# Hyena stage: both directions' filters multiplied once in two halves of the array, their sum and difference formed on VectorE, and the weights' low parts subtracted on GpSimd

## The reference, cut to what matters

```python
def hyena_mixer(h, w_in, b_in, short_w, short_b, w1, b1, w2, b2, w3, freq, filt_bias, w_out, b_out):
    L = h.shape[1]
    u = centred_depthwise_conv(h @ w_in + b_in, short_w, short_b)
    v, x1, x2 = jnp.split(u, 3, axis=-1)
    filt = hyena_filters(L, w1, b1, w2, b2, w3, freq)
    z = x1 * two_sided_fft_conv(v, filt[:, 0, 0], filt[:, 0, 1], filt_bias[0])
    z = x2 * two_sided_fft_conv(z, filt[:, 1, 0], filt[:, 1, 1], filt_bias[1])
    return z @ w_out + b_out
```

## Time and profile before

| | us |
|---|---|
| median of three executions | 2646.16 |
| lowest, highest | 2643.12, 2646.53 |
| the profiled execution's own time | 2648.7 |
| its span | 2646.3 |
| PE busy | 2461.9 (93%) |
| DVE busy | 1141.1 (43%) |
| ACT busy | 773.5 (29%) |
| POOL busy | 51.5 (2%) |

### The profile page before, as it was taken

How to read it: one execution, slowest core, us unless ns; L and a number is a source line. 1 busy time by engine, 2 the same in 40 slices (tenths; PEclk the granted TensorE clock), 3 DMA queues, 4 the chain that set the end, 5 groups by cost and what they waited for, 6 DMA issues and landing times. The chain is left out here.

```text
span 2646.3 us, 39564 instructions
## 1 busy us (share of the span) xinstructions
PE 2461.9 (93%) x16812; PEld 1555.6 (59%) x16812; DVE 1141.1 (43%) x2226; ACT 773.5 (29%) x1602; POOL 51.5 (2%) x68
## 2 busy tenths in 40 slices
PE   8989999999899999978799999998999969988887
PEld 7856888888678888855443334344767743322222
DVE  4456543333788989886300000002556542211113
ACT  4346433333433333223311111112347522110002
POOL 0000000000000000000200000000000010000000
PEclk9979999999999999987899999999999979999999
DMA  5240332222210101025799999997230479999996
GB/s 205 97 153 29 143 116 96 96 96 96 94 50 33 50 33 50 32 112 203 313 383 397 377 384 386 393 384 320 101 159 2 191 258 367 428 428 428 427 428 284
DMA packets 58103, 570.49 MB, mean 216 GB/s; under 512 B 6815, under 2 KB 15015, under 8 KB 24776
## 3 DMA queue, kind: packets, MB, share of 16 engines
q1 hardware_dynamic: 50904, 544.37, 51.5%
q0 software_dynamic: 5584, 18.35, 2.2%
q10 hardware_dynamic: 1440, 5.24, 0.5%
HBM read 554.84 MB, written 13.11 MB: 215 GB/s over the span
## 5 line engine op out<-in xcount | busy, mean ns | idle before, releaser
L2973 PE MATMUL moe_gate<-ring,moe_xe_l 128*32 128x512 f32 (+1 forms) x1240 | 192.6, 599 | 17.8 <-DMA ring<-in_moe_gu 11.9
L3960 DVE SCALAR_TENSOR_TENSOR moe_hidden<-moe_hidden,moe_gate_rows,moe_up 128x512 f32<-128x512 f32 x31 | 23.2, 747 | 400.4 <-ACT moe_hidden L3883 400.4
L2973 PE MATMUL moe_up<-ring,moe_xe_l 128*32 128x512 f32 (+1 forms) x1240 | 190.2, 594 | 0.0
L3988 DVE SCALAR_TENSOR_TENSOR residual<-experts_psc,mod,residual 128x512 f32<-128x512 f32 (+1 forms) x76 | 53.3, 707 | 283.9 <-PE experts_psc L3824 169.1
L3744 PE MATMUL experts_py_l<-ring,experts_turn_l 128*32 128x512 f32 (+1 forms) x1136 | 141.3, 593 | 3.5 <-DMA ring<-in_moe_down 2.8
L1019 DVE TENSOR_TENSOR mlp_w_lo<-ring,mlp_w_hi 128x512 fp32r<-128x512 f32 x144 | 96.7, 688 | 97.8 <-ACT mlp_w_hi L964 97.6
L3883 ACT ACTIVATE moe_hidden<-moe_gate 128x512 f32<-128x512 f32 x31 | 18.5, 597 | 360.2 <-PE moe_up L2973 360.2
L964 ACT CAST mlp_w_hi<-ring 128x512 fp32r<-128x512 f32 x144 | 86.4, 618 | 123.5 <-PE mlp_acc L920 123.5
L2973 PEld LDWEIGHTS moe_up<-ring,moe_xe_l 128*32 128x32 f32 (+1 forms) x1240 | 49.7, 115 | 108.2 <-issue 108.2
L2973 PEld LDWEIGHTS moe_gate<-ring,moe_xe_l 128*32 128x32 f32 (+1 forms) x1240 | 44.8, 115 | 99.9 <-issue 70.1
L918 PE MATMUL mlp_acc<-mlp_h_hi,mlp_w_hi 128*128 128x512 f32 x256 | 100.0, 391 | 0.0
(11 more groups left out here) (678 smaller groups left out, 5210.5 us busy)
## 6 DMA issues: line engine op xcount, KB each, us to landing
ring<-in_moe_gu SPq DMA_DIRECT2D x91, 2048.0 KB, 11.3
ring<-in_moe_down SPq DMA_DIRECT2D x45, 2048.0 KB, 9.8
ring<-in_ada_w SPq DMA_DIRECT2D x24, 2048.0 KB, 8.6
ahead_wide_early<-in_moe_gu SPq DMA_DIRECT2D x9, 2048.0 KB, 30.5
ahead_wide_high<-in_moe_gu SPq DMA_DIRECT2D x9, 2048.0 KB, 30.5
ahead_wide_low<-in_moe_gu SPq DMA_DIRECT2D x9, 2048.0 KB, 30.4
normed<-in_moe_gu SPq DMA_DIRECT2D x9, 2048.0 KB, 30.5
ring<-in_w_up SPq DMA_DIRECT2D x8, 2048.0 KB, 7.4
```

Of the source, the lines that this page charges most:

```text
L2973: last = core.nc.tensor.matmul(banks[m][at:at + n, :], xe_l[:, e, k, a:a + n], columns(2 * kk + m, FH * half, FH), start=(k == 0), stop=(k ...
```

## The change

- **Filters.** `w3` becomes [128, 2, 256]: forward weights in rows 0 to 63, backward in rows 64 to 127. `filters` takes two tiles at a time and issues four products of 64 rows and 256 columns: for each tile one in the upper and one in the lower half of the array, with two banks, one for the forward and one for the backward filter.
- **Taps.** `make_taps` multiplies two tiles of one direction in one operation (six operations of 512 elements per order, as before). The new function `sides` forms the sum, then the difference as -2 times the backward taps plus the sum, both in place and linked, and adds the bias row on one partition. It is called for taps 0 to 3 and for taps 4 and 5.
- **Waits.** A counter `taps_made` (four a turn) takes the place of `sp_free` for what needs the finished taps: the first unit of `transform` waits for the first call of `sides`, the third unit for the second. SP's reloads wait for it too. TensorE's `filters` wait for `win_loaded` instead of for ScalarE.
- **ScalarE.** `turn_filters_round` goes; its four uses with it.
- **Low parts.** `weights_low` for turns 0 and later (36 subtractions of 128x512) moves from VectorE's program to GpSimd's queue: pieces 4 and 5 of the turn before at the head of a turn, pieces 0 to 3 behind the wait for `project(it - 1, 5)` and, from turn 1 on, for `outwards(it - 1)`.
- **SP.** One DMA less per turn (four instead of five, and `at_zero`).

```diff
-w3 = st.sb("w3", [P, 2, 2, QC])
+w3 = st.sb("w3", [P, 2, QC])
...
-turned_round = st.counter("hy_filters_turned_round", TURNS)
+taps_made = st.counter("hy_filters_turned_round", 4 * TURNS)
...
-win_loaded = st.counter("hy_win_loaded", 96 * TURNS)
+win_loaded = st.counter("hy_win_loaded", 80 * TURNS)
...
+def taps_at(it, o, first):
+    return taps_made.at(4 * it + 2 * o + (2 if first else 1))
...
         for q in range(TURNS):
...
-                sp.wait_ge(sp_free.handle, sp_free.at(4 + spec_at(q - 1, 18 + 5)))
+                sp.wait_ge(taps_made.handle, taps_at(q - 1, 1, 4))
             last_layer = ins["hy_ffn_w3_2"].rearrange("a (o d c) -> a o d c", o=2, d=2)[:, :, :, q * QC:(q + 1) * QC]
             sp.dma_start(win[:], core.consts["window"][:, :, q * QC:(q + 1) * QC]).then_inc(win_loaded.handle, 16)
             for s in range(2):
-                sp.dma_start(w3[0:64, :, s, :], last_layer[:, :, 0, :]).then_inc(win_loaded.handle, 16)
-            sp.dma_start(w3[64:P, :, 0, :], last_layer[:, :, 1, :]).then_inc(win_loaded.handle, 16)
+                sp.dma_start(w3[64 * s:64 * (s + 1), :, :], last_layer[:, :, s, :]).then_inc(win_loaded.handle, 16)
             sp.dma_start(at_zero[:], ins["hy_bias_rows"][:, 0, q * QC:(q + 1) * QC]).then_inc(win_loaded.handle, 16)
             if q == 0:
...
-            sp.wait_ge(sp_free.handle, sp_free.at(4 + spec_at(q, 5)))
+            sp.wait_ge(taps_made.handle, taps_at(q, 0, 4))
             sp.dma_start(at_zero[:], ins["hy_bias_rows"][:, 1, q * QC:(q + 1) * QC]).then_inc(win_loaded.handle, 16)
...
         def filters(it, o, some=range(6)):
-            for t in some:
-                b = take_spec(it, 18 * o + t)
-                nc.tensor.matmul(b[:], h2[:, t * P:(t + 1) * P], w3[:, o].rearrange("p s n -> p (s n)"), start=True, stop=True).then_inc(sp_done.handle, 1)
-
-        def transform(it, m0, src):
+            for t in some[::2]:
+                both = [take_spec(it, 18 * o + t + s) for s in range(2)]
+                for i in range(2):
+                    for s in range(2):
+                        side = slice(64 * s, 64 * (s + 1))
+                        last = nc.tensor.matmul(both[s][:, i * QC:(i + 1) * QC], h2[side, (t + i) * P:(t + i + 1) * P], w3[side, o, :], start=True, stop=True, tile_position=(64 * s, 0))
+                        if i:
+                            last.then_inc(sp_done.handle, 1)
+        def transform(it, m0, src, made):
...
+                    if a == 0 and s in made:
+                        pe.wait_ge(taps_made.handle, made[s])
...
         def spectra(it, o):
-            pe.wait_ge(sp_free.handle, sp_free.at(4 + spec_at(it, 18 * o + 5)))
-            transform(it, 18 * o + 6, lambda a: taps[:, a])
+            transform(it, 18 * o + 6, lambda a: taps[:, a], {0: taps_at(it, o, 0), 2: taps_at(it, o, 4)})
...
             if it == 0:
-                pe.wait_ge(turned_round.handle, turned_round.at(1))
+                pe.wait_ge(win_loaded.handle, win_loaded.at(64))
                 filters(0, 0)
...
             if full:
-                pe.wait_ge(turned_round.handle, turned_round.at(it + 2))
+                pe.wait_ge(win_loaded.handle, win_loaded.at(80 * (it + 1) + 64))
                 filters(it + 1, 0, range(4))
...
+        def weights_low(it, i):
+            for half in range(2):
+                pool.wait_ge(w_high.handle, w_high.at((it + 1) * 2 * NP + 2 * i + half + 1))
+                n = chunk(it, i)
+                nc.gpsimd.tensor_tensor(piece(core.slot_low(n), i, 4 * half, 4), piece(core.slot(n), i, 4 * half, 4), w_hi[:, (2 * i + half) % W_BUFS],
+                                        ALU.subtract).then_inc(w_low.handle, 1)
...
         for it in range(TURNS):
+            if it:
+                weights_low(it - 1, 4)
+                weights_low(it - 1, 5)
+            else:
+                pool.wait_ge(w_low.handle, w_low.at(2 * NP))
...
+                for i in range(4):
+                    weights_low(it, i)
                 await_item(pool, it, "proj", 3)
...
-        def turn_filters_round(it):
-            act.wait_ge(win_loaded.handle, win_loaded.at(96 * it + 80))
-            nc.scalar.activation(w3[64:P, :, 1, :], w3[64:P, :, 0, :], ACT.Identity, scale=-1.0).then_inc(turned_round.handle, 1)
...
-        turn_filters_round(0)
...
-                turn_filters_round(it + 1)
...
         def make_taps(it, o, some=range(6)):
-            for t in some:
+            for t in some[::2]:
                 m = 18 * o + t
-                if t == 5:
-                    dve.wait_ge(sp_free.handle, sp_free.at(4 + spec_at(it, m - 1)))
-                    if o:
-                        dve.wait_ge(win_loaded.handle, win_loaded.at(96 * (it + 1)))
-                    zero = taps[0:1, 0, 0:5:4, :]
-                    link(nc.vector.tensor_tensor(zero, zero, at_zero[:].unsqueeze(1).to_broadcast([1, 2, QC]), ALU.add))
-                dve.wait_ge(sp_done.handle, sp_done.at(spec_at(it, m)))
-                nc.vector.tensor_tensor(taps[:, :, t, :], spec[m % 4][:].rearrange("p (s n) -> p s n", s=2), win[:, t].unsqueeze(1).to_broadcast([P, 2, QC]),
-                                        ALU.mult).then_inc(sp_free.handle, 1)
+                dve.wait_ge(sp_done.handle, sp_done.at(spec_at(it, m + 1)))
+                for s in range(2):
+                    last = nc.vector.tensor_tensor(taps[:, s, t:t + 2, :], spec[(m + s) % 4][:].rearrange("p (t n) -> p t n", t=2), win[:, t:t + 2, :], ALU.mult)
+                    last.then_inc(sp_free.handle, 1)
+        def sides(it, o, first, n):
+            dve.wait_ge(sp_free.handle, sp_free.at(4 + spec_at(it, 18 * o + first + n - 1)))
+            ahead, behind = [taps[:, s, first:first + n, :] for s in range(2)]
+            link(nc.vector.tensor_tensor(ahead, ahead, behind, ALU.add))
+            link(nc.vector.scalar_tensor_tensor(out=behind, in0=behind, scalar=-2.0, in1=ahead, op0=ALU.mult, op1=ALU.add))
+            dve.wait_ge(win_loaded.handle, win_loaded.at(80 * (it + 1) if o else 80 * it + 64))
+            zero = taps[0:1, 0, first, :]
+            nc.vector.tensor_tensor(zero, zero, at_zero[:], ALU.add).then_inc(taps_made.handle, 1)
...
-            dve.wait_ge(win_loaded.handle, win_loaded.at(96 * it + 80))
+            dve.wait_ge(win_loaded.handle, win_loaded.at(80 * it + 64))
             if it == 0:
                 make_taps(0, 0)
+                sides(0, 0, 0, 4)
+                sides(0, 0, 4, 2)
                 convolve(0, 2)
                 convolve(0, 3)
...
                 make_taps(it, 0, range(4, 6))
                 add_out(it - 1, 4)
                 add_out(it - 1, 5)
+                sides(it, 0, 0, 4)
                 add_out(it - 1, 6)
+                sides(it, 0, 4, 2)
                 add_out(it - 1, 7)
                 convolve(it, 2)
             for s in range(6):
                 combine(it, 6, s, pq)
-                if it and s % 3 < 2:
-                    weights_low(it - 1, 4 + s // 3, s % 3)
             for s in range(6):
                 combine_tokens(it, 12, s, ab)
             dve.wait_ge(sp_free.handle, sp_free.at(4 + spec_at(it, 17)))
             products(it, 0, 0)
             products(it, 0, 1)
-            if full:
-                weights_low(it, 0, 0)
-                weights_low(it, 0, 1)
             gates(it, 0)
             make_taps(it, 1, range(4))
+            sides(it, 1, 0, 4)
             convolve(it, 4)
             convolve(it, 5)
             make_taps(it, 1, range(4, 6))
+            sides(it, 1, 4, 2)
             for s in range(6):
                 combine(it, 24, s, pq)
-                if full and s % 3 < 2:
-                    weights_low(it, 1 + s // 3, s % 3)
...
-            if full:
-                weights_low(it, 3, 0)
-                weights_low(it, 3, 1)
             products(it, 1, 1)
             gates(it, 1)
             gated_low(it)
```

## The result

The changed kernel takes 2670.66 us (median of 6 executions, 2664.66 to 2674.09) against 2645.98 us for the kernel before beside it (6, 2639.09 to 2650.51): ratio 1.0093, 95% interval 1.0077 to 1.0109, 24.7 us slower by the medians. The forecast was +20 and 2666, with 2644 to 2681 as the range. The profiled execution took 2671.57 us, span 2669.7.

The account below looks back on a forecast made before the run. TensorE bounds where VectorE idles, and VectorE where TensorE idles, so their two meetings a turn decide. +4.9 us for sums and filters plus +15 for GpSimd's collisions made +20: 2666 us against the median, range 2644 to 2681.

Parts of the forecast that it names:

- the change of shape: TensorE's filters: 0.20 us lost when the array shape changes, about 0.16 on entry, 0.36 us a call.
- The rival of halves that don't overlap: TensorE's filters stay as long as before plus shape changes, 1.9 us a turn: 2659 us, chance 5%.
- The walk of the sums: Hyena stage step by step, GpSimd free of side effects: turn 0 and both meetings summed to +4.9 us.
- Meeting 1: After the output projections, TensorE waits for VectorE's adds to `residual` before the first transforms: +2.05 us per turn, turns 1-3.
- Meeting 2: Second transforms of a turn, where TensorE needs VectorE's taps: -0.95 us in turns 1 and 2, -1.2 in turn 3.
- what was taken out between the combinations is worth nothing: VectorE's subtractions removed between its combinations gain nothing, since VectorE follows TensorE step by step there.
- One GpSimd subtraction, 0.92 us: GpSimd's time for one two-input 128x512 subtraction, set at 0.92 us with 2.4 us as upper bound.
- The collision: VectorE stands still for each GpSimd subtraction met: six a turn, behind first `back` and before second transforms, 5.1 us; +15 us.
- The row of 0.96 us: VectorE's 128x768 products just behind `project(it-1, 5)`: expected to grow from 0.96 to near 1.9 us if GpSimd's reads collide.
- GpSimd is slow: Rival: 1.7 us a GpSimd subtraction, six costing 9.8 us a turn, 29 in all: 2680 us, chance 11%.
- Faster: Rival: sums fit VectorE's gaps, the wait for `residual` doesn't grow, TensorE's 15 us come through: 2631 us, chance 9%.
- GpSimd is free: Rival: GpSimd's subtractions don't disturb VectorE, leaving only +5 us: 2651 us, chance 30%.

Follow-up runs that it names:

- run 1: The changed kernel with the 36 low-part subtractions back on VectorE in their old places: 2657.0 us, ratio 1.0044 to the kernel before.
- run 6: The changed kernel with GpSimd's 36 subtractions replaced by writes of zero: 2649.8 us, ratio 1.0010 to the kernel before.
- run 5: The changed kernel with GpSimd's 36 subtractions replaced by one-input copies of the same size: 2658.5 us, ratio 1.0047 to the kernel before.
- run 8: The changed kernel with all subtractions on VectorE and VectorE's sums and convolutions reordered: 2643.8 us, ratio 0.9996 to the kernel before.
- run 2: The kernel before with only the 36 low-part subtractions moved to GpSimd, filters and taps unchanged: 2651.5 us, ratio 1.0023.

## Why the prediction was right

The sign and the mechanism held: GpSimd's reads lengthen VectorE's two-input operations, and the second `back` waits for them. That the size came so near, +24.7 for +20, is in part luck: the stage itself is 28.1 us longer, and some 4 us came back behind it with the clock.

- **Filters.** 2.08 and 1.22 us forecast, 2.00 and 1.13 measured; the row from filters to second `back` is 1.93 us in run 1 against 3.43 before, a gain of 1.50 where 1.36 was forecast. Of the 0.36 us a call for the change of shape, 0.16 stands in no row; by these lengths it was some 0.08 too high. The rival of halves that don't overlap is out. (Its 2659 us leaves GpSimd's 15 us out; with them it would have been 2674.)
- **Sums.** 4.1 us more VectorE work per order: they measure 2.9 (1.22, 1.23, 0.41) and 1.8 us a call, as forecast.
- **The walk of the sums, +4.9: mis-sized in the stage.** Run 6 measures +10.6 there, by turns +4.0, -0.3, +3.0 and +4.0 (by the medians +3.1, which doesn't contradict 4.9). Run 1, for which +8 was expected, measures +12.7 (stage +14.8), and shows where. At turn 0 the forecast had +1.8 and run 1 has +4.8: the stage's first transforms start 12.79 us behind the first filter product, where before it was 9.55, at a granted clock of 0.50 where it was 0.74, and the stretch behind them is 2.04 us longer, at 0.95. Meeting 1 is +1.62 a turn, under the 2.05 forecast, but I costed a wait at its length only. In the 31 us behind it the granted clock is 0.95 (second row of run 1) and that stretch is 1.54 longer. Meeting 2 came to -1.9 (filters -1.50, then -0.43), better than the -0.95; but "what was taken out between the combinations is worth nothing" let me miss the opposite: TensorE, two microseconds ahead by then, meets a VectorE that is late, and from the second transforms to `back` turn 1 has 33.35 (at 0.95) instead of 30.28 and turn 2 32.42 (at 1.00) instead of 29.93. The gain at meeting 2 was given back in the next stretch.
- **One GpSimd subtraction, 0.92 us: mis-sized.** It measures 1.25 us undisturbed (four in 5.00) and 1.53 in the mean. The figure from the Trainium skill's GPSIMD Engine Reference, 3.1, an estimate of 1.12 us, was nearer than mine.
- **The collision.** "VectorE stands still for each subtraction it meets", at the places named: the products behind the first `back`, and the convolutions and sums before meeting 2. The row of 0.96 us went to 1.91, as the last part of the prediction asked. A turn was forecast at 5.1 us, and at the places named it shows 4.03 + 1.09 = 5.1 of lengthened operations. That is luck: a subtraction costs VectorE more than the 0.92 set, and of the six named only five lengthen anything. Two places were missed. Piece 3, laid on slack, lengthens the second order's products by 2.07 us, and from the second transforms to `back` the change has 31.44 us against 30.42 in run 6; pieces 4 and 5, laid on VectorE's idle wait, cost the split of `hyena_u` 0.74. Over the stage the reads cost 17.5 us against run 6, where 15 was forecast; a part of it is the clock behind the second `back` (15.50 us at 0.89 against 13.87 at 1.00). Against run 1 13.4 us reach the end, by turns 5.8, 2.5, 3.4 and 1.8.
- **The lock.** The Trainium skill, SBUF — State Buffer, section "SBUF: two separate sides", says that GpSimd and VectorE hold a shared port pair as an exclusive lock, also against a VectorE operation with two SBUF inputs. The section has this only against a GpSimd operation that reads SBUF, and run 6 agrees: writes cost nothing. The traces agree in kind where both read two inputs, 1.01 us being lost for each subtraction. For a copy they don't fit a lock over the whole operation: 0.29 to 0.41 us is lost, where a copy alone lasts 0.61.
- The rivals: "GpSimd is slow" was right about one thing, that a subtraction that collides takes 1.7 us, and wrong that VectorE loses as much. "Faster" fell though its condition was met: the sums before add 6 take 2.86 us, just under the 3 us named (and so did my own 2.92), and the wait grew all the same, from 0.53 to 2.71 us, because those before add 7 count too. "GpSimd is free" fell by the sign that was named for it: the row of 0.96 us didn't stay.

What stays open: why the clock falls after some waits of the same length and not after others. At meeting 1 of turn 1 the change and run 1 both wait 1.8 us; run 1's next twelve records take 4.44 us, the change's 2.76.

## What to carry to other kernels

Before a step is moved from VectorE to GpSimd to relieve VectorE, list what VectorE runs at that moment: where both read SBUF with two inputs, each GpSimd operation can cost VectorE more than VectorE would have needed for the work itself (here 1.0 us against 0.6), at a place that was not chosen. Here 36 subtractions of 0.6 us left VectorE, and 23.8 us of delay came. Where two engines meet twice a turn, a saving on one of them is worth only what the other can follow, up to the next meeting; add the stretches of a whole turn, not only those around the edit. And try the order of the late engine's list before judging an edit: here it was worth 11 us without one instruction more or less.

## What the runs showed of the hardware

- GpSimd's `tensor_tensor` of 128x512 float32 from SBUF: 1.25 us, 1.75 us where VectorE reads two SBUF operands beside it. A copy of that size is 0.61 us where VectorE is idle (956.20 us in run 5) and 0.88 in the mean, a write 0.53 (18.5 us for 36). VectorE needs 0.68 for the same subtraction, 0.6 from start to start.
- VectorE's operations with an operand from PSUM beside GpSimd's subtractions kept their length: the gate at 840.64 us takes 1.11 us (1.09 before) with a subtraction beside all of it (840.57 to 841.86), and the tap multiplications at 922.36 us 0.68 each, as before.
- A wait can cost more than its length. After the wait of 3.80 us the next stretch of 15.5 us ran at 0.89 and was 1.63 us longer than in run 1, where there is no wait and the clock is 1.00 (13.87 us). The kernel before has 1.00 in all five stretches of the turn, and so has run 8. It isn't so after every wait: in run 2 the second `back` waits 2.28 us in turns 0, 1 and 2, and the stretch to the next filters takes 12.77 us at 0.87, 11.16 at 1.00 and 12.78 at 0.87.
- Two products of 64 rows, one in each half of the array, run side by side: sixteen records of 256 columns hold TensorE for 1.93 us at full clock (895.12 to 897.05 in run 1), where sixteen in sequence at 0.216 us, by the earlier trace rows, would be 3.46.
